# Feed-forward up of a hybrid encoder layer: seven block products in two passes

## What is computed

```python
D_MODEL, SEQ, DEC_SEQ, D_FF, CONV_W = 1024, 2048, 32, 2816, 3
def conv_ffn(h, conv_state, w_up, w_conv, b_conv, w_down):
    u = h @ w_up                                   # (tokens, 1024) @ (1024, 5632)
    padded = jnp.concatenate([conv_state.astype(u.dtype), u], axis=1)
    uc = sum(padded[:, j:j + T] * w_conv[j] for j in range(CONV_W)) + b_conv
    a, g = jnp.split(uc, 2, axis=-1)
    out = (jax.nn.silu(a) * g) @ w_down
    return out, padded[:, -(CONV_W - 1):]
```

## Time and profile before

| | us |
|---|---|
| median of 3 runs | 3188.12 (3183.26 to 3189.86) |
| span of the profiled execution | 3185.2 |
| feed-forward up in it, first to last matmul | 1643.7 to 2646.1 |
| TensorE busy in the span | 3070.3 (96%) |
| VectorE busy | 1534.5 (48%) |
| ScalarE busy | 1093.8 (34%) |
| GpSimd busy | 763.5 (24%) |

### The profile page before, as it was taken

The page is one execution under the profiler, slowest core; times in us unless marked ns, Lnnn a source line. Parts: engine busy times, 40 slices in busy tenths (PEclk is TensorE's granted clock), DMA queues, the critical chain, the costliest instruction groups (busy, mean ns, idle before and its releaser), DMA issues.

```text
span 3185.2 us, 46250 instructions
## 1 busy us (share of the span) xinstructions
PE 3070.3 (96%) x17742; PEld 2679.4 (84%) x17742; DVE 1534.5 (48%) x1951; ACT 1093.8 (34%) x2163; POOL 763.5 (24%) x678
## 2 busy tenths in 40 slices
PE   7999998998999999899999999999999999999998
PEld 5788887776777887788889999999999997887886
DVE  2300035522998998685655343434443436224221
ACT  5611122213777787344552121211212123113110
POOL 3311013212666776220111111111111114002000
PEclk8999999998999999999999999999999999999999
DMA  6322224424522330885651111011111125434332
GB/s 216 110 67 77 73 83 136 138 96 117 128 56 55 84 76 11 274 279 188 216 192 39 53 53 53 27 53 53 53 30 49 53 82 187 157 125 157 124 130 68
DMA packets 251064, 336.13 MB, mean 106 GB/s; under 512 B 58845, under 2 KB 171033, under 8 KB 244125
## 3 DMA queue, kind: packets, MB, share of 16 engines
q1 hardware_dynamic: 234718, 284.75, 29.4%
q0 software_dynamic: 14864, 49.31, 4.6%
q10 hardware_dynamic: 1332, 0.06, 0.0%
HBM read 225.16 MB, written 108.89 MB: 105 GB/s over the span
## 4 chain that ended last, share of the span: by engine, by line
PE 55%; DVE 2%; DMA 1%; issue 1%; ACT 1%; SPq 0%; POOL 0%; ACTq 0%; DVEq 0%; POOLq 0%
PE facc L2157 30%; PE dacc L2185 15%; PE eacc L2137 6%; PE mpT L2205 1%; PE mpm L2215 1%; PE mpD L2196 1%; PE eyT L2120 0%; PE mpS L2225 0%; PE exT L2150 0%; DMA dfreed_plain<-w_down 0%; PE mpN L2241 0%; PE mpT L2256 0%; PE mpN L2245 0%; DVE fV L1918 0%; DVE fV L1914 0%
## 5 line engine op out<-in xcount | busy, mean ns | idle before, releaser
L2157 PE MATMUL facc<-fh,fwH 128*128 128x416 f32 x3520 | 947.3, 350 | 0.0
L2157 PEld LDWEIGHTS facc<-fh,fwH 128*128 128x128 f32 x3520 | 660.5, 188 | 5.6 <-issue 0.3
L2157 PE MATMUL facc<-fh,fwL 128*128 128x416 f32 x1760 | 618.5, 351 | 0.0
L708 PE MATMUL pacc<-pring,h1H 128*128 128x512 f32 x1360 | 436.0, 397 | 9.3 <-POOL pring L576 5.9
L1082 POOL TENSOR_TENSOR aS<-aS,aC 128x512 f32<-128x512 f32 (+3 forms) x326 | 334.7, 1034 | 165.8 <-DVE aC L1042 156.6
L1042 DVE TENSOR_TENSOR_SCAN aC<-aB,aC,a 128x512 f32<-128x512 f32 (+3 forms) x326 | 362.8, 1113 | 21.6 <-ACT aB L1000 10.3
L1717 ACT ACTIVATE fU<-facc 128x416 f32<-128x416 f32 (+1 forms) x220 | 112.7, 513 | 754.8 <-PE facc L2157 754.7
L1914 DVE TENSOR_SCALAR fV<-fU,fcw,fcb 128x2048 f32<-128x2048 f32 (+2 forms) x90 | 116.3, 1334 | 527.8 <-ACT fU L1719 510.1
L2185 PE MATMUL dacc<-dfreed 128*128 128x512 f32 (+1 forms) x1340 | 322.4, 398 | 11.3 <-DVE dfreed L1962 8.7
L2157 PEld LDWEIGHTS facc<-fh,fwL 128*128 128x128 f32 x1760 | 330.6, 188 | 1.6
L1594 POOL TENSOR_TENSOR fwL<-fraw,fwH 128x1024 fp32r<-128x1024 f32 x44 | 134.2, 3053 | 816.1 <-ACT fwH L1708 816.1
(11 more groups left out here) (295 smaller groups left out, 4203.6 us busy)
## 6 DMA issues: line engine op xcount, KB each, us to landing
proj_out<-pstage SPq DMA_DIRECT2D x119, 256.0 KB, 2.0
dfreed_plain<-act_d SPq DMA_DIRECT2D x20, 1408.0 KB, 6.3
fraw<-w_up SPq DMA_DIRECT2D x44, 512.0 KB, 5.6
act_d<-fV SPq DMA_DIRECT2D x21, 1024.0 KB, 5.3
qk_T<-pturn POOLq DMA_DIRECT2D x68, 256.0 KB, 3.0
mwa<-w_ada SPq DMA_DIRECT2D x16, 1024.0 KB, 5.7
dthird_plain<-act_d SPq DMA_DIRECT2D x11, 1408.0 KB, 6.3
praw<-w_in SPq DMA_DIRECT2D x56, 256.0 KB, 2.8
```

Of the source, the lines that this page charges most:

```text
L708: op = mm_(acc[:, n % NB], h[:, kk, tok(t)], weight(q, w), start=(j == 0), stop=(j == len(order) - 1))
L2157: mm = nc.tensor.matmul(dst, a[:, j, kk], b[w][:, kk], start=(kk == 0 and m == 0), stop=(kk == KD - 1 and m == 2))
```

## The change

The 2080 tokens are cut into a first pass of 1248 (ranges 0 to 2) and a second of 832 (ranges 3 and 4). In each pass two ranges and the two tiles F and G of a pair, with the contraction cut in two halves of 4 chunks, form a 2 by 2 by 2 block product. It is made in seven products P1 to P7 of 12 matmuls each (Strassen's scheme in the form with shared sums), not eight; range 0 of the first pass stays as it was (`std_f`, `std_g`, 24 matmuls each). A pair has 132 matmuls in the first pass and 84 in the second, and the 22 pairs run twice, so each weight tile is loaded and split twice.

What the scheme needs beside that:
- for each pair and pass four sums of weight half-tiles, 128x512 (VectorE `sum_one` to `sum_four`), each made high by ScalarE (`high_sum`) and low by GpSimd (`low_sum`). GpSimd's `prepare` is now: low half of F, four low sums, low half of G (in the second pass only the half of G that is used);
- for each pass four sums of h2 blocks of 128x1664 (T1 to T4, VectorE), each made high (ScalarE `high_t`) and low (VectorE `low_t`), and three plain blocks B11, B21, B22 (high ScalarE `high_block`, low GpSimd `low_block`). That stands before the first pair of each pass, and the products of that pair (`seven`) wait for the blocks one by one;
- partial results that are used twice: ScalarE copies bank a to bank b (`seed_b`), bank b to bank c (`seed_c`) and P5's bank to SBUF (`take_e`); VectorE makes the two results of the last range as PSUM plus E (`take_c22`, `take_c12`). P4 waits for `take_c22`, P6 and P2 for `seed_b`, P7 and P3 for `seed_c`.

The convolution is made over 1248 tokens in one piece in the first pass (`conv_wide`), and over 800 + 32 in the second (`conv_narrow`); two rows are kept between the passes in `hist`. In each slot VectorE first finishes G and the product of the pair before, then does sums and takes, then F of its own pair. `first_rows`, of which 18 of the 22 rows can be loaded only while the last pair runs, is followed by GpSimd for 10 rows and by VectorE for 12 (before: GpSimd for all). Act tile 0 comes whole from the first pass. The ring for the second half's rows has 6 buffers, not 8. The diff, cut to its core:

```diff
@@ feed-forward constants
-    NR = 8
+    WIDE, NARROW = 3 * WT, 2 * WT
+    NR = 6
...
+            def next_up(g, i):
+                sp.wait_ge(w_low[F], g + 1)
+                sp.wait_ge(sums_ready, 4 * g + 4)
+                load_up(i, F)
+                sp.wait_ge(w_low[G], g + 1)
+                load_up(i, G)
@@ block.gpsimd
+            def prepare(g, last):
+                low_half(F, g)
+                for n in range(4):
+                    low_sum(n, g)
+                low_half(G, g, slice(KH, KD) if last else slice(0, KD))
...
+            b_first = (blocks[:, 0:KH, 0:WT], blocks[:, KH:KD, 0:WT], blocks[:, KH:KD, WT:])
+            low_block(B11, b_first[0], 1)
+            low_sum(0, 0)
+            low_sum(1, 0)
+            low_block(B21, b_first[1], 2)
+            store_h2(final)
+            low_sum(2, 0)
+            low_block(B22, b_first[2], 3)
+            low_sum(3, 0)
@@ block.scalar
+            def narrow_slot(g, width):
+                seed_b(g, False)
+                silu(g - 1, width)
+                take_e(g)
+                seed_c(g)
+                take_c11(g, 2)
+                high_half(F, g + 1, True)
+                for n in range(4):
+                    high_sum(n, g + 1)
+                take_c21(g, 2)
+                high_half(G, g + 1, True)
@@ block.vector
+            def sum_one(g):
+                for j in range(2):
+                    dve.wait_ge(raw_in[j], 16 * g + 16)
+                at_least(dve, s_low, 4 * g - 3)
+                v.tensor_tensor(tmp[:, 0], g1, g2, ALU.add).then_inc(sums_ready, 1)
...
+            def take_c22(g, at, narrow=False):
+                dve.wait_ge(done["P7"], g + 1)
+                dve.wait_ge(e_taken, g + 1)
+                for to, a, b in halves_of(narrow, at):
+                    op = v.tensor_tensor(U[:, G, to:to + b - a], bank_b[:, a:b], E[:, a:b], ALU.add)
+                op.then_inc(c22_taken, 1)
...
+            def narrow_slot(g, i):
+                conv_narrow(g - 1, i - 1, G)
+                product(g - 1, NARROW)
+                sum_one(g + 1)
+                sum_two(g + 1)
+                take_c22(g, 2 + WT, True)
+                sum_three(g + 1)
+                take_c12(g, 2 + WT, True)
+                sum_four(g + 1)
+                conv_narrow(g, i, F)
...
+            g = NF - 1
+            conv_wide(g - 1, g - 1, G)
+            product(g - 1, WIDE)
+            dve.wait_ge(blocks_in, 32)
+            dve.wait_ge(h_in, 32)
+            dve.wait_ge(done["P5"], NF)
+            v.tensor_tensor(plain(T1), late_blocks[:, 0:KH], plain(B11), ALU.subtract).then_inc(t_ready, 1)
@@ block.tensor
-            def up(q, j, w):
-                dst = up_acc[:, bank(q, w), 0:WT]
-                for kk in range(KD):
-                    for m, (a, b) in enumerate(((upH, hH), (upH, hL), (upL, hH))):
+            def three(bank, left, at, begins, sem):
+
+                count = left[0].shape[1]
+                for kk in range(count):
+                    for m, (a, b) in enumerate(((left[0], at[0]), (left[0], at[1]), (left[1], at[0]))):
...
+            def p4(g):
+                pe.wait_ge(w_low[G], g + 1)
+                pe.wait_ge(c22_taken, g + 1)
+                three(bank_b, weight(G, behind), block_of(T4), False, done["P4"])
+
+            def wide_pair(g):
+                p1(g, True)
+                p5(g)
+                p6(g)
+                p2(g)
+                std_f(g)
+                p7(g)
+                p3(g)
+                p4(g)
+                std_g(g)
+
+            def narrow_pair(g):
+                p1(g, False)
+                p5(g)
+                p6(g)
+                p2(g)
+                p7(g)
+                p3(g)
+                p4(g)
...
+            seven(0, 0, 0)
+            with pe.Fori(1, NF) as i:
+                wide_pair(i)
+            seven(NF, 3, 4)
+            with pe.Fori(1, NF) as i:
+                narrow_pair(NF + i)
```

More of the change, by code:

```diff
@@ L1372, in mlstm_output_ffn @@
[L1372 to L1383, removed]
+        stdH, stdL = std[:, 0], std[:, 1]
@@ new lines, in _ @@
+            high_block(B22, blocks[:, KH:KD, WT:])
+            high_t(T4, 3)
+            seed_c(0)
+            high_t(T3, 4)
+            high_sum(2, 0)
+            high_sum(3, 0)
+            for u in range(2):
+                act.wait_ge(h2_stored[u], 16 * len(range(u, NT, 2)))
+            take_e(0)
+            take_c11(0, 2 + WT)
+            take_sf(0)
+            high_half(F, 1)
+            for n in range(4):
+                high_sum(n, 1)
+            take_c21(0, 2 + WT)
+            take_sg(0)
@@ L1810, in _ @@
+            g = 2 * NF - 1
+            seed_b(g, False)
+            silu(g - 1, NARROW)
+            act_high(0)
+            take_e(g)
+            seed_c(g)
+            for kk in range(4):
+                first_high(kk)
+            take_c11(g, 2)
+            for kk in range(4, 16):
+                first_high(kk)
+            take_c21(g, 2)
+            silu(g, NARROW)
+            for kk in range(16, NF):
+                first_high(kk)
             for n in range(1, SWITCH + 1):
@@ L1868, in tile_slot @@
             def tile_slot(i):
-                if isinstance(i.t, int) and i.t == NPT:
-                    low_h(1)
                 if i.within(2):
@@ new lines, in _ @@
+            v.memset(U[:, :, 0:2], 0.0).then_inc(history_set, 1)
+            sum_one(1)
+            sum_two(1)
+            take_c22(0, 2 + 2 * WT)
+            sum_three(1)
+            take_c12(0, 2 + 2 * WT)
+            sum_four(1)
+            dve.wait_ge(b_low, 3)
+            dve.wait_ge(history_set, 1)
+            conv_wide(0, 0, F)
+            with dve.Fori(1, NF - 1) as i:
+                wide_slot(i)
+            g = NF - 1
+            conv_wide(g - 1, g - 1, G)
+            product(g - 1, WIDE)
@@ new lines, in _ @@
+            conv_wide(g, g, G)
+            product(g, WIDE)
+            low_t(T4, 8, 8)
+            g = NF
+            sum_one(g + 1)
+            sum_two(g + 1)
+            take_c22(g, 2 + WT, True)
+            sum_three(g + 1)
+            take_c12(g, 2 + WT, True)
+            sum_four(g + 1)
+            conv_narrow(g, 0, F)
+            with dve.Fori(1, NF - 1) as i:
+                narrow_slot(NF + i, i)
+            g = 2 * NF - 1
+            conv_narrow(g - 1, NF - 2, G)
+            product(g - 1, NARROW)
```

842 lines of the change are left out of this document (502 added, 340 removed).

## The result

| | before | after |
|---|---|---|
| time, median (lowest to highest) | 3185.94 (3181.42 to 3189.90) us | 3196.26 (3192.72 to 3200.23) us |
| ratio | | 1.0032, interval 1.0022 to 1.0042 |
| span of the profiled execution | 3185.2 us | 3198.5 us |
| TensorE busy, share, instructions | 3070.3 us, 96%, 17742 | 3009.9 us, 94%, 17216 |
| VectorE busy, share, instructions | 1534.5 us, 48%, 1951 | 1958.1 us, 61%, 2517 |

The change makes the kernel 0.3% slower: 528 matmuls of up are gone (the counts differ by 526, as the kernel after starts two PSUM banks with a matmul each, line 2626), TensorE is busy 60 us less, and the median is 10.3 us higher. The forecast was 3178 us, 0.3% faster. The time lies in the predicted range, on the other side of no change.

What follows compares the result with a forecast made beforehand. TensorE's matmuls bound the kernel before; VectorE and GpSimd taking turns would bound the new second pass. Up 45 + 496.6 + 66 + 384.3 = 992 (-10.5), its end -3, switch +3: span 3175, time 3178 us; range 3152 to 3216.

Steps and rivals of the forecast that it cites:

- Rival 1: Second pass: TensorE stays the bound, 15.8 us a slot, 52.5 us less, time 3126 us; 8%, partial form (about 3158) 12%.
- Rival 2: Second pass: turn-taking costs its full sum, 20.0 us a slot, +36 us, 3213 us; decides from 18.8 a slot; 25%.
- Narrow slots: Second pass, 21 steady slots: VectorE and GpSimd taking turns give 18.3 us a slot, bounds 17.2 and 20.5.
- Wide slots: First pass, 20 steady slots: TensorE stays the bound at 24.8 us a slot, 496.6 us in all.
- Between the passes: Slots 21 and 22: queued loads and block sums make them 66 us, range 58 to 74; TensorE alone needs 40.6.
- First pair: Start of the first pass: 24.8 us of matmuls plus 20 of waits for blocks, 45 us, range 40 to 52.
- End of up: From up's end to down(1): 22.4 us, 3 us won; bounds 8 lost more or 3 less.
- The switch: Wait ahead of down(18), 3.44 us before: the ring of 6 adds 3 us, between 0 and 6.
- What the profile was to show: First-pass slots 24.8 us without idle; second-pass 18.3, idle ahead of P4, VectorE and GpSimd almost always busy; 25 us border hole.
- Rival 3: Start of first pass and between passes: blocks cost 15 us more together, each a chain over four engines; 3193 us; 15%.
- The chance of 0.32 for slower: Whole kernel slower than before: 25% from Rival 2 plus 7% from Rival 3.

Runs made afterwards that it cites:

- the first experiment: Kernel after, with GpSimd's six subtractions per steady second-pass slot cut to two columns and two low parts filled by ScalarE copies: slots 15.95 us, span 3132.9 us.
- e2_sp_orders: Kernel after, with B11 and B21 loads ahead of store_wide(20), and act tile 2 and gate-row loads ahead of up's last store: 3181.71 us, ratio 0.9995 to before.
- the changed kernels of the table: Kernel after, its rerun, with SP's orders moved, and with a plain second pass: down(1) to down(18) 267.0, 265.3, 260.4 and 259.8 us; before 260.3.
- plain form: Kernel after, with the second pass as eight products without sums, SP's orders moved and down(0)'s rows reordered: 3150.15 us, ratio 0.9897 to before.
- the kernel changed again: The kernel after run once more, unchanged: 3193.27 us, ratio 1.0027 to before.

## Why the sign was wrong

**The mechanism was right.** VectorE and GpSimd take turns, and their sum bounds the second pass. The forecast slot was 18.3 us, the measured one 18.52; without GpSimd's part it is 15.95. Rival 1, TensorE as the bound (15.8), falls: it needs GpSimd's subtractions taken away, as in the first experiment. Rival 2, slower through turn-taking in full, falls as well: it decides from 18.8 a slot, and its 20.0 did not come. (Its own terms, 11.8 + 7.7 + 0.1, add up to 19.6, not 20.0.) That a take beside a GpSimd subtraction keeps its length holds here too: L2087 at 2299.67 took 0.64 us with GpSimd's 3.42 beside it. The Trainium skill, SBUF — State Buffer, section "Who interferes with whom", states as a rule that the two engines share one port pair as an exclusive lock, and the first experiment agrees (VectorE's busy time falls from 18.1 to 12.1 us a slot).

**The step that failed is the sum: its terms in up and at its end were undersized, and one was missing.** The forecast had 10 us to give away, 0.3%. No single term turns the sign; all but one erred the same way:

- *Narrow slots:* 18.52 for 18.3, 21 times: +4.5. The work of VectorE was counted as 11.8 and is 12.1, the turns as 6.4 and are 6.0. The rest is idle time of VectorE, 0.4 a slot. The slot is 2.6 us longer than TensorE's own 15.95: 1.6 are idle and 0.9 are matmuls that take longer, most of it at a lower clock (0.97 in the mean of that stretch, see the last section).
- *Wide slots:* 25.01 for 24.8, 20 times: +3.7. That the first pass would stay with TensorE was right. A pair of before is 45.21 us, 0.1884 a matmul, not 0.188: 0.8 us over the 20 slots; the other 2.8 come with the products of 12, left open above.
- *Between the passes:* 68.7 for 66. The step was right in its parts: the loads behind `store_wide(20)`, VectorE idle 7 us (7.43), T1 17 us after slot 20's end (17.5). VectorE needed some 2 us more from there to the take of slot 22. e2_sp_orders shows the step in the other direction: from the take of slot 20 to that of slot 22 it is 67.9 us there, 74.5 in the kernel after.
- *First pair:* 47.3 for 45, but not as I summed it. I had 24.8 us of matmuls and 20 of waits (the four named add up to 19). TensorE's idle times there are 3.58, 2.23, 0.34, 1.14, 3.92 and 2.51, together 13.7 us; it was at work in the other 33.6, 8.8 more than for 132 matmuls in a steady slot. Some 1.4 of that are the transposes of the last tile and the two matmuls of line 2626; most of the rest is the clock. The table by stretch, from the end of P7 to P4 of the first pair:

```profile
1685.00:1695.00 10.00, 7.49 (x22) 6.65 (x22) 8.66 (x6) 1.90 (x3) 10.00 (x5) 0.50 0.01 2
```

  22 matmuls in 7.49 us are 0.34 each, at a granted 0.50, the level of 1.2 GHz, with the idle times of 3.92 and 2.51 us ahead of and among them: 3.3 us more than at full clock in this stretch alone. I had not priced the clock at all; that two errors nearly cancelled is luck.
- *End of up:* down(1) was to come 3 us sooner and came 0.8 sooner. VectorE's order was right, but of its rows of down(0) the first four took 1.16 us each, with GpSimd's rows beside them, and the last eight 0.61, where I had 0.58. This step was undersized by 2.
- *The switch:* +3 was forecast; 1.9 to 2.9 for the ring alone, -0.5 to 2.6 in the changed kernels of the table with down(2)'s stall taken off. This term was the one that came under.
- *down(2):* **the missing term.** I followed SP's queue at the border of the passes and priced it, and did not follow it past up's end. There `load_act(2)` stands behind up's last store. It costs 4.1 and 4.2 us in the two traces of the kernel after and had no term and no rival. It and the clock are what the forecast left out altogether; the other steps were wrong in size. Even without it the sum would be some 4 us above before.

Together: 13 us in up, 2 at its end, 4 in down(2). On the -10.5 of the forecast's sum this gives some +9 us; the two spans give +7.7 without the later start of up, the medians +10.3, and +8.0 when it was run again.

**What the profile was to show** came, but for one point: VectorE is busy 98% in the second pass, GpSimd not "almost all the time" but 58%. In each slot it waits 6.9 to 8.5 us for a high part from ScalarE (6.96 in the rows above). It is the sum of the two that fills the slot: only VectorE's record shows it, as GpSimd's turns lie inside VectorE's instructions.

**Rival 3**, the blocks dearer by 15 us, was the nearest in its result (3193) and wrong in its place: the blocks cost 5 us more, not 15. The chance of 0.32 for slower looks too low for a margin of 10 us on a sum with seven terms: what I had left out of them (hand-overs, the clock, a queue) adds to the time.

**What would have shown it before.** The forecast itself says that the second pass gets slots of 18.3 where 96 plain matmuls need 96 x 0.188 = 18.05. The scheme's own second pass was a loss by my own numbers (slots longer by 0.25 us, and 25 us for its blocks), and I compared it only with the sum of both passes.

## What to carry to other kernels

A scheme that trades matmuls for sums pays in a stage only where its slot, the larger of TensorE's time and of VectorE's and GpSimd's added, stays below the plain form's. In wide slots VectorE with the turns in it is busy 19.7 us (0.789 of 25.01), below TensorE's 25.0, and 144 plain matmuls would take 27.1, an estimate from the 0.1884 of before: a gain. In narrow ones it is busy 18.1 against TensorE's 15.95, and the slot of 18.52 is longer than the plain form's 18.13: a loss. Price each pass by itself against its plain form before summing. When the forecast gain is smaller than one store in front of one load, follow each queue to the next stage's first wait, or call the sign open.

## What the hardware showed that I had not expected

- The turns add almost exactly (12.1 us of VectorE's own work and 6.0 of turns in a slot of 18.52) and reach the smallest instructions: a copy of two columns on VectorE takes 0.16 us alone and 1.27 beside a 512-column subtraction of GpSimd.
- TensorE's granted clock can fall around single idle times of a few us, and the matmuls then take nearly twice their time, until it is back. The table by stretch of the kernel after, at the border of the passes (the first stretch is idle but for two matmuls, the second is P7 and P3 of slot 22 after 6.96 us of idle), and TensorE's first two matmuls of P4 in slot 21, 1.03 us where two take 0.54 in a steady slot:

```profile
2215.00:2227.00 12.00, 0.29 (x2) 0.00 (x0) 11.86 (x5) 8.15 (x9) 9.30 (x3) 0.60 0.02 8
2252.00:2258.00 6.00, 5.65 (x16) 5.49 (x17) 5.86 (x3) 1.58 (x3) 2.96 (x1) 0.50 0.00 0
```

```profile
2227.79 1.03 PE L2422 MATMUL facc<-fright,fwH 128*128 128x416 f32 x2 [12.50 <-DVE fU L2087]
```

  Shorter ones are enough: in the narrow slots of the kernel after, TensorE is idle 2.3 to 2.4 us at P4 eleven times, and nine times a stretch at 0.50 begins within 1.3 us behind it; twice none does. The first line below is such a stretch, behind an idle time of 2.35 us; the second is at full clock although 3.52 us of idle stand right ahead of it.

```profile
2320.00:2323.00 3.00, 3.00 (x10) 2.90 (x9) 2.95 (x6) 1.33 (x3) 3.00 (x3) 0.50 0.01 2
2264.00:2270.00 6.00, 6.00 (x33) 5.92 (x32) 5.87 (x9) 2.69 (x5) 5.82 (x4) 1.00 0.31 90
```

  So the idle time alone does not tell whether the clock falls, nor do the first two matmuls: in the kernel changed again two of them after 3.94 us of idle in the first pair took 0.61 us, and the stretch from 1679 to 1682 us just behind them is granted 0.50.
- A satisfied wait and an increment in the middle of a product cost nothing that shows (45.21 us a pair with and without). Yet a wide slot with seven products of 12 takes 0.14 us more than 132 x 0.1884, and the slot of the experiment without turns 0.12 more than 84 x 0.1884: 0.02 us a product. This stays open.
